# Strips for head values and norm sums, FFN on the unnormed stream, and a finer wait in the joint FFN

## The reference, cut to what matters

```python
# _rms, rms_norm: y = x * rsqrt(mean(x*x) + eps) [* g]
# first block, layer 1: MLA, 16 heads, 96 query/key features (64 + 32 rotated), 64 value features
q = _rms(q.reshape(..., MLA_HEADS, MLA_QK)) * q_gain          # then rope on the last 32
k = _rms(concat([k_nope, k_rope])) * k_gain
p = softmax(einsum('bqhd,bkhd->bhqk', qi, k) * scale); o = einsum('bhqk,bkhd->bqhd', p, v)
# first block: FFN of both streams (layer 0: latent and context together)
(gelu(_dwconv(g, conv_w, conv_b)) * val) @ w_out
# second block, each of two layers
x = x + rms_norm(m, norm_mix_post[l])
h = rms_norm(x, norm_ffn_pre[l]); g, u = split(h @ w_gate_up)
x = x + rms_norm((silu(g) * u) @ w_down, norm_ffn_post[l])
```

## Time and profile before

| what | value |
|---|---|
| median of 3 runs | 4068.17 us (4064.98 to 4074.45) |
| the profiled execution | 4073.31 us, span 4071.5 us |
| mean granted TensorE clock | 0.974 |
| PE / DVE / ACT / POOL busy | 3828.8 / 1573.8 / 1502.7 / 1263.9 us |
| weight chunks | 520, 512 KB each |

### The profile page before, as it was taken

How to read it: one execution, slowest core, us unless ns; L and a number is a source line. 1 busy time by engine, 2 the same in 40 slices (tenths; PEclk the granted TensorE clock), 3 DMA queues, 4 the chain that set the end, 5 groups by cost and what they waited for, 6 DMA issues and landing times.

```text
span 4071.5 us, 57748 instructions
## 1 busy us (share of the span) xinstructions
PE 3828.8 (94%) x21980; PEld 3044.7 (75%) x21980; DVE 1573.8 (39%) x2404; ACT 1502.7 (37%) x2500; POOL 1263.9 (31%) x524
## 2 busy tenths in 40 slices
PE   6998999999987999999979999989998999998998
PEld 4865688888865777788857778868886777876886
DVE  2423454242325555344336554331116655223112
ACT  3324432121244444333245554332225555323222
POOL 2530033232330000244423223434442332343443
PEclk8999999999998999999989999999999999999999
DMA  4344421111120000122212112222221111222222
GB/s 180 114 177 160 168 87 67 57 62 62 62 78 16 16 15 19 66 102 98 98 63 68 67 64 77 95 68 98 98 98 62 63 68 68 78 88 72 98 97 84
DMA packets 84702, 333.78 MB, mean 82 GB/s; under 512 B 9520, under 2 KB 9648, under 8 KB 78000
## 3 DMA queue, kind: packets, MB, share of 16 engines
q1 hardware_dynamic: 83808, 329.22, 23.3%
q10 hardware_dynamic: 720, 2.10, 0.2%
HBM read 329.18 MB, written 2.10 MB: 81 GB/s over the span
## 4 chain that ended last, share of the span: by engine, by line
PE 63%; issue 26%; POOL 6%; DVE 3%; ACT 2%; POOLq 0%; DVEq 0%; ACTq 0%
PE pB L1895 13%; PE pB L276 12%; PE pB L278 12%; PE pB L277 12%; POOL w_lo L2415 6%; PE pO L1509 2%; PE pS L408 2%; PE pB L1491 1%; PE pS L1925 1%; PE pS L1491 1%; PE pT L1501 1%; PE pT L1953 1%; PE pO L1975 1%; PE pO L1980 1%; PE pS L1930 0%
## 5 line engine op out<-in xcount | busy, mean ns | idle before, releaser
L2415 POOL TENSOR_TENSOR w_lo<-w_raw,w_hi 128x1024 fp32r<-128x1024 f32 x520 | 1263.6, 2431 | 2780.8 <-ACT w_hi L314 2780.3
L276 PE MATMUL pB<-h_hi,w_hi 128*128 128x512 f32 x2080 | 825.7, 397 | 51.0 <-POOL w_lo L2415 17.4
L278 PE MATMUL pB<-h_hi,w_lo 128*128 128x512 f32 x2080 | 815.9, 392 | 0.0
L277 PE MATMUL pB<-h_lo,w_hi 128*128 128x512 f32 x2080 | 815.2, 392 | 0.0
L314 ACT ACTIVATE w_hi<-w_raw 128x1024 fp32r<-128x1024 f32 x520 | 548.9, 1056 | 499.2 <-PE pB L278 326.9
L276 PEld LDWEIGHTS pB<-h_hi,w_hi 128*128 128x128 f32 x2080 | 395.5, 190 | 143.6 <-issue 50.4
L277 PEld LDWEIGHTS pB<-h_lo,w_hi 128*128 128x128 f32 x2080 | 395.2, 190 | 85.1 <-issue 4.3
L278 PEld LDWEIGHTS pB<-h_hi,w_lo 128*128 128x128 f32 x2080 | 394.5, 190 | 83.5
L276 PE MATMUL pB<-b_hi,w_hi 128*128 128x512 f32 (+1 forms) x1120 | 424.6, 379 | 16.1 <-DVE xb_lo L675 10.3
L278 PE MATMUL pB<-b_hi,w_lo 128*128 128x512 f32 (+1 forms) x1120 | 411.4, 367 | 0.0
L277 PE MATMUL pB<-b_lo,w_hi 128*128 128x512 f32 (+1 forms) x1120 | 411.1, 367 | 0.0
(11 more groups left out here) (464 smaller groups left out, 5140.4 us busy)
## 6 DMA issues: line engine op xcount, KB each, us to landing
w_raw<-stream SPq DMA_DIRECT2D x520, 512.0 KB, 3.2
under<-ada SPq DMA_DIRECT2D x42, 1024.0 KB, 4.8
arena<-ada SPq DMA_DIRECT2D x6, 1024.0 KB, 18.7
x<-xT SPq DMA_DIRECT2D x1, 2048.0 KB, 9.5
out<-x SPq DMA_DIRECT2D x8, 256.0 KB, 2.0
xc<-cT SPq DMA_DIRECT2D x1, 1024.0 KB, 10.4
arena<-bmask ACTq DMA_DIRECT2D x1, 1024.0 KB, 5.4
arena<-brope ACTq DMA_DIRECT2D x2, 256.0 KB, 5.9
```

What stands on the lines that cost most here:

```text
L276: pe.matmul(dst, lh, rh, start=(begin and k == 0), stop=False)
L277: pe.matmul(dst, lh, rl, start=False, stop=False)
L278: last = pe.matmul(dst, ll, rh, start=False, stop=(end and k == len(pairs) - 1))
L2415: pool.tensor_tensor(w_lo[:, s, :], w_raw[:, s, :], w_hi[:, s, :].bitcast(F32), ALU.subtract).then_inc(lo_ready, 1)
```

## The change

The MLA heads are rewritten. A pair of heads is the unit of order: its eight units of scores, maximum, exponential and transposes run with "turns" of the next pair between them (`turns_beside`: Q, K, C projections, SQ, SK, SC sums, V values). Turns use two PSUM banks alternately. The turned probabilities of the whole pair are kept, and one AV turn makes the weighted values with the values as the stationary side, head 0 on output partitions 0 to 63 and head 1 on 64 to 127; an R turn spreads the reciprocals of the row sums. The result is already feature by token, so the transposes at the end go. In the weight stream the key/value chunk of a group moves from third to second.

For ten norms the squares go to four buffers, tiles 0 to 3 and 4 to 6 are summed on 32 output partitions each, ACT copies the partial sums scaled by 1/32, and one product of them and one of the eighth tile's squares finish. In the second block the FFN's first product runs on x times the gain; DVE multiplies the gate's sums by rstd before Silu and the finished output by rstd. In the joint FFN the first result chunk waits tile by tile. The high/low query source moves from one pair of buffers to another. Parts left out: the other turns, the ACT loop over units (the same order as the DVE loop shown, with copy, exponential and the weight splits of the next chunks in slots 4 and 6) and declarations.

```diff
+        def act_strip_square(act, name, kt, src, n, ready):
+            base = N_BASE[NORMS.index(name)]
+            act.wait_ge(*ready)
+            act.wait_ge(sq_used, base + (4 if kt >= 4 else 0))
+            act.activation(sq_strip[kt % 4][:, 0:n], src(kt), ACT.Square).then_inc(sq_ready, 1)
+        def act_strip_part(act, name, n):
+            c = NORMS.index(name)
+            act.wait_ge(rstd_ready, c)
+            act.wait_ge(sq_used, N_BASE[c] + KD - 1)
+            act.activation(rt[:, 0:n], pS[:, 512:512 + n], ACT.Copy, scale=1.0 / 32).then_inc(part_ready, 1)
...
+        def pe_strip_sums(pe, name, k0, k1, n):
+            c = NORMS.index(name)
+            pe.wait_ge(rt_ready, c)
+            pe.wait_ge(sq_ready, N_BASE[c] + k1)
+            for kt in range(k0, k1):
+                r = 32 * (kt % 4)
+                last = pe.matmul(pS[r:r + 32, 512:512 + n], ones[:, 0:32], sq_strip[kt % 4][:, 0:n], start=(kt < 4), stop=(kt + 4 >= KD - 1))
+            last.then_inc(sq_used, k1 - k0)
+        def pe_strip_end(pe, name, n):
+            pe.wait_ge(part_ready, STRIPS.index(name) + 1)
+            pe.matmul(pS[:, 0:n], ones, rt[:, 0:n], start=True, stop=False)
+            pe.wait_ge(sq_ready, N_BASE[NORMS.index(name)] + KD)
+            pe.matmul(pS[:, 0:n], ones, sq_strip[3][:, 0:n], start=False, stop=True).then_inc(sq_used, 1)
...
+                elif m == KD - 1:
+                    pe_chunk(pe, g0 + m, src, width, n, kts, lambda: pe_strip_sums(pe, name, 4, KD - 1, n))
                 else:
                     pe_chunk(pe, g0 + m, src, width, n, kts)
-                if m:
-                    pe_square_sum(pe, name, m - 1, n)
-            pe_square_sum(pe, name, KD - 1, n)
+                if m == 4:
+                    pe_strip_sums(pe, name, 0, 4, n)
+            pe_strip_end(pe, name, n)
...
+        def pe_joint_first(pe, g, j0, nj):
+            s = g % SLOTS
+            pe_wait_chunk(pe, g)
+            for kt in range(nj):
+                pe.wait_ge(act_lo, j0 + kt + 1 + SLOTS)
+                pe_three(pe, bank[s][:, 0:T], [(wt(s, kt), rows(*B, T, kt, 0, T))], kt == 0, kt == nj - 1)
+            pe_three(pe, ctx_bank[s], [(wt(s, kt), rows(*XB, C, kt, 0, C)) for kt in range(nj)]).then_inc(chunk_done, 1)
...
-                pe.wait_ge(act_lo, j0 + nj + SLOTS)
+                pe_joint_first(pe, g0, j0, nj)
...
+        def pe_scaled_chunks(pe, g, name):
+            for e in range(2):
+                pe_wait_chunk(pe, g + e)
+            for kt in range(KD):
+                if kt == 5:
+                    pe_strip_sums(pe, name, 0, 4, T)
+                if kt == KD - 1:
+                    pe_strip_sums(pe, name, 4, KD - 1, T)
+                    pe_strip_end(pe, name, T)
+                pe.wait_ge(*normed(name)(kt))
+                for e in range(2):
+                    s = (g + e) % SLOTS
+                    last = pe_three(pe, bank[s][:, :], [(wt(s, kt), rows(*H, T, kt, 0, T))], kt == 0, kt == KD - 1)
+                    if kt == KD - 1:
+                        last.then_inc(chunk_done, 1)
...
-                        act.wait_ge(act_lo, v(j + (call * F_TILES + 1)))
-                        act.activation(cbuf[:, s, 0:n], bank[g % SLOTS][:, 0:n], ACT.Silu).then_inc(evac[g % SLOTS], 1)
+                        act.wait_ge(*ev(g))
+                        act.activation(cbuf[:, s, 0:n], cbuf[:, s, 0:n], ACT.Silu).then_inc(gelu_ready, 1)
...
+                        dve.wait_ge(chunk_done, done(g))
+                        dve.wait_ge(act_lo, v(J + 1))
+                        dve.tensor_tensor(cbuf[:, s, 0:n], bank[g % SLOTS][:, 0:n], rstd, ALU.mult).then_inc(evac[g % SLOTS], 1)
+                        dve.wait_ge(gelu_ready, v(J + 1))
...
+                    dve.tensor_tensor(fm, bank[(m + g0) % SLOTS][:, :], fm, ALU.add).then_inc(f_whole, 1)
+                    dve.wait_ge(f_whole, v(m + (l * KD + 1)))
+                    dve.tensor_tensor(fm, fm, rstd, ALU.mult).then_inc(evac[(m + g0) % SLOTS], 1)
...
+        def turns_beside(p):
+            a, b, g = 2 * p + 2, 2 * p + 3, p // 2
+            if p + 1 == PAIRS_A:
+                return [[] for _ in range(8)]
+            if p % 2:
+                return [[("Q", a)], [("K", a), ("C", p + 1)], [("SQ", a), ("SK", a)], [("SC", p + 1), ("Q", b)], [("K", b)], [("SQ", b)],
+                        [("SK", b)], []]
+            return [[("Q", a)], [("K", a), ("C", p + 1)], [("K", b), ("V", 3 * g)], [("V", 3 * g + 1), ("V", 3 * g + 2)],
+                    [("SQ", a), ("SK", a), ("SC", p + 1)], [("Q", b)], [("SQ", b), ("SK", b)], []]
+        FIRST_TURNS = [("Q", 0), ("K", 0), ("C", 0), ("SQ", 0), ("SK", 0), ("SC", 0), ("Q", 1), ("K", 1), ("SQ", 1), ("SK", 1)]
+        TURNS_A = list(FIRST_TURNS)
+        for _p in range(PAIRS_A):
+            if _p:
+                TURNS_A += [("AV", _p - 1), ("R", _p - 1)]
+            for _row in turns_beside(_p):
+                TURNS_A += _row
+        TURNS_A += [("AV", PAIRS_A - 1), ("R", PAIRS_A - 1)]
...
+            elif what == "AV":
+                pe.wait_ge(a_ca, 8 * n + 8)
+                pe.wait_ge(a_cd, 8 * n + 8)
+                pe.wait_ge(va_copied, 3 * (n // 2) + 3)
+                for kt in range(6):
+                    for e in range(2):
+                        h = (2 * n + e) % 4
+                        src = th_low[e][:, kt, :] if kt < 3 else th_high[e][:, kt - 3, :]
+                        last = pe.matmul(dst[64 * e:64 * e + 64, :], va[:, kt, h * 64:h * 64 + 64], src, start=(kt == 0), stop=(kt == 5))
+                last.then_inc(av_done, 1)
+            else:
+                pe.wait_ge(rows_ready, n + 1)
+                for t in range(TB):
+                    for e in range(2):
+                        c = (8 * n + e * TB + t) % 16
+                        last = pe.matmul(dst[64 * e:64 * e + 64, t * P:(t + 1) * P], ars[:, c:c + 1].to_broadcast([P, 64]), ident,
+                                         start=True, stop=True)
+                last.then_inc(rows_done, 1)
...
+        def pe_unit_scores(pe, u):
+            n, t = u // TB, u % TB
+            if u >= 2:
+                pe.wait_ge(a_e, u - 1)
+            pe.wait_ge(head_ready, n + 1)
+            lhs = qf[0:QK_A, n % 4, t * P:(t + 1) * P]
+            pe.matmul(score[u % 2][:, 0:512], lhs, kf[0:QK_A, n % 4, 0:512], start=True, stop=True)
+            pe.matmul(score[u % 2][:, 512:TC], lhs, kf[0:QK_A, n % 4, 512:TC], start=True, stop=True).then_inc(a_s, 1)
+        def pe_unit_turn(pe, u):
+            pe.wait_ge(a_e, u + 1)
+            pe.wait_ge(a_ca, u)
+            pe.wait_ge(a_cd, u)
+            for k in range(6):
+                o = k * P if k < 3 else 512 + (k - 3) * P
+                last = pe.transpose(pT[:, o:o + P], attP[:, u % 2, k * P:(k + 1) * P], ident)
+            last.then_inc(a_t, 1)
...
+            for p in range(PAIRS_A):
+                if p:
+                    pe_turn(pe, ("AV", p - 1))
+                    pe_turn(pe, ("R", p - 1))
+                for s, beside in enumerate(turns_beside(p)):
+                    u = 8 * p + s
+                    pe_unit_turn(pe, u)
+                    for turn in beside[:-1]:
+                        pe_turn(pe, turn)
+                    if u + 2 < UNITS:
+                        pe_unit_scores(pe, u + 2)
+                    for turn in beside[-1:]:
+                        pe_turn(pe, turn)
+            pe_turn(pe, ("AV", PAIRS_A - 1))
+            pe_turn(pe, ("R", PAIRS_A - 1))
+            pe.wait_ge(a_e, UNITS)
+            pe.wait_ge(rows_done, PAIRS_A)
+            pe.sem_inc(o_turned, KD)
...
+        def dve_pair_rows(dve, p):
+            dve.wait_ge(a_e, 8 * p + 8)
+            dve.wait_ge(rows_done, max(p - 1, 0))
+            o = p % 2 * 8
+            dve.reciprocal(ars[:, o:o + 8], asum[:, o:o + 8]).then_inc(rows_ready, 1)
+        def dve_pair_scale(dve, p):
+            dve.wait_ge(av_done, p + 1)
+            dve.wait_ge(rows_copied, p + 1)
+            dve.tensor_tensor(o_row, bank_of(("AV", p)), o_row, ALU.mult).then_inc(av_scaled, 1)
+        def dve_pair_low(dve, p):
+            dve.wait_ge(o_hi, p + 1)
+            o = slice(p * T, (p + 1) * T)
+            dve.tensor_tensor(b_lo[:, o], o_row, b_hi[:, o].bitcast(F32), ALU.subtract).then_inc(o_lo, 1)
...
+            for p in range(PAIRS_A):
+                if p:
+                    dve_pair_scale(dve, p - 1)
+                for s, beside in enumerate(turns_beside(p)):
+                    u = 8 * p + s
+                    dve_unit_copy(dve, u)
+                    if s == (4 if p % 2 else 5) and p + 1 < PAIRS_A:
+                        dve_head(dve, 2 * p + 2)
+                    for turn in beside[:-1]:
+                        dve_turn(dve, turn)
+                    if u + 2 < UNITS:
+                        dve_unit_max(dve, u + 2)
+                    for turn in beside[-1:]:
+                        dve_turn(dve, turn)
```

(51 more changed lines are left out.)

583 lines of the change are left out of this document (298 added, 285 removed).

## The result

| | before | after |
|---|---|---|
| median | 4066.91 us (4 runs, 4064.98 to 4074.45) | 4014.15 us (4 runs, 4013.31 to 4016.01) |
| ratio | | 0.9866, 95% interval 0.9854 to 0.9879 |
| span of the profiled execution | 4071.5 us | 4014.2 us |
| mean granted TensorE clock | 0.974 | 0.973 |

The gain is 52.8 us. I had forecast 130, with 3905 to 3978 as the range: right in sign, far off in size.

What follows compares the result with a forecast made beforehand. TensorE, busy 94% of the span, bounds the kernel. Gains 83 (heads) + 24.5 + 15 + 12 - 1.5 = 133 us gave 3940 from the profiled execution, 3935 from the median; 3 given back: 3938, range 3905 to 3978.

Steps and rivals of the forecast that it cites:

- the first and last pair: Heads: eight pairs at 38.1 us, 1.5 of waiting each; last pair's chain of some 3 us hidden under the first output chunk.
- the start: Head stage: no units to hide in, so some 6 us of waits for the first head's chain.
- PE's work in a pair: Heads: PE work of 38.1 us per pair, 305 for eight, against a period of 49.1 per pair before.
- the bound: Heads, weighted values: a pair costs 10.3 us if the two 64-wide strips don't overlap, 5.2 if they do.
- I get no wait in most slots: Heads: PE waits 0.5 to 2 us per pair behind the second query; taken as 1.5, bounds 0 and 6.
- Norm sums: Norm sums in 32-wide strips: a round about 1.0 us, each norm gains 3.5, seven norms 24.5 us.
- Joint FFN: First result chunk of the joint FFN taken tile by tile: ready tiles cover the wait, gaining 15 us.
- Unnormed stream: Second block's FFN: third chunk earlier, gaining 12 us for both layers, less 1.5 for added DVE products.
- Rival 1: Heads: turns' round trips not hidden, 4 to 6 us lost per pair; 3958 to 3974, say 3966; chance 0.20.
- Rival 2: Values and norm sums: strips don't overlap, 4012 us, or only in part, 3951; chance 0.08.
- Rival 3: Heads: their chain becomes the bound, 59 us a pair, 4090 in all, deciding from 56 a pair; chance 0.02.
- I weighed 9 us by it against 3: Strips: 52 tiling-mode changes at 0.17 us would take 9 us; forecast took 0.1 per exit, 3 in all.

Runs made afterwards that it cites:

- the best order: Changed kernel with head's finish behind the maximum, weight splits in the last slot, last key's roots behind the next copy, query rope two slots behind its gain: 3960.02 us.
- the fourth of the heads' runs: Changed kernel with head's finish behind the maximum, rope behind the next slot's maximum, weight splits in the last slot, last key's roots behind the next copy: 3980.34 us.

## Why the prediction was wrong, step by step

Nearly all of what is missing lies in the heads. Their stage was to take 323 us and took 391.5; in the best order it takes 336.9. So 54.6 of the 68.5 us are the order of the queues, 13.9 the first and last pair, the start and small terms.

- *PE's work in a pair, 38.1 us*: right. With the queues in a better order a pair is 40.2 us at full clock, 38.8 of work and 1.4 of waits, against 38.1 + 1.5. The values at 5.2 and the reciprocals at 1.3 measured 5.18 and 1.00, and 10.33 for the former in one strip, as the bound had it.
- *"I get no wait in most slots and 0.5 to 2 us per pair behind the second query; I take 1.5, bounds 0 and 6."* This is the step that failed. The waits measured 5.4 and 7.0 us, 6.2 on average, and the clock took 2.6 more, which I had not priced at all: 47.8 for a pair, 7.6 over what the same instructions need in another order. (The expectation of the fourth of the heads' runs has 3.5 us for the clock; the granted clock gives 3.4 in the odd pairs and 1.7 in the even ones.) I had followed the turns' round trips, but not what is queued ahead of the unit's own maximum and copy: the head's finish, the roots and the splits. I had even written that POOL may hold up DVE inside the heads' chain, and gave 3 us back for it; moving the splits alone, which frees both DVE and ACT, brought 15.6. That loads and POOL's subtractions "are the same" was true of their number; their place was part of the cost.
- *The first and the last pair.* I let every unit cost its 1.95 us and every pair lose 1.5. In the best order the stage is 336.9 us and not 323. Of the 14 us between, 7 are in the first pair: 40.1 us from its first transposes to its values, with 31.6 of work since no pair stands before it, one wait of 2.8 us and 3.4 us of lower clock behind it. Another 3.5 are in the last pair, whose units have no turns beside them, so that PE waits for DVE's and ACT's copies (0.87, 1.65 and 1.57 us; 20.6 us for eight units, where I had 15.6 + 1.5). Some 3 are in the six pairs between (40.1 against 39.6). The start came out as written (22.6 us).
- *Norm sums, 24.5 us for seven norms, 3.5 each*: right in the round (0.99 against my 1.0) and near in the sum: 31.6 for nine norms is 3.5 each, 3.2 behind the heads. In the last norm of a layer the strips won 3.1 us and the new product of output and rstd took 2.3 of them away.
- *Joint FFN, 15 us*: 13.2.
- *Unnormed stream, 12 - 1.5 = 10.5 us*: 4.1 by the medians, 1.4 by the traces. The first product came 4.9 us after the first update, where I had 4.8, but the third chunk came 26.9 us after it instead of 21.6. The term missed that ACT's squares share a queue with its high parts and wait for a round placed a tile too late (2.21 us, and 1.7 by the clock behind it), and that the product of output and rstd is of the kind that POOL holds (2.31 for 0.69); for its added products I had 0.75 us a layer, and they took 2.3.
- *Rival 1* was the right one in kind: lateness on DVE delays the maximum and the exponential, 4 to 6 us a pair; it had no term for the clock, 2.6 us a pair, and stopped at 3974. The clock in six pairs is some 16 of the 40 us from there to the result; the rest is the waits being over its 6 in the even pairs, the first and last pair and the unnormed stream. Rival 2's number was near the result and its mechanism is refuted. Rival 3's "56 us a pair" was not reached.
- *Two statements of the Trainium skill.* The Trainium skill (TensorEngine Tiling, Key Properties) says that a change of tiling mode drains the engine; I weighed 9 us by it against 3. Entering and leaving a round together cost 0.13 us here (0.99 for 0.86), so the trace stays with the smaller. The Trainium skill (TensorE: Matmul & The Clock Gate, Part 3) measured 2.38x for three column tiles. Here two strips of 64 gave the full factor (5.18 against 10.33 us), and four tiles in 32-wide strips took 0.99 us with entering and leaving, where four full-wide sums are 3.4.
